# Two-layer decoder trunk: key chunks of the second layer turned by VectorE blocks and DRAM in place of TensorE

## What is computed

```python
def hgrn2_layer(h, norm_gain, w_in, o_gain, w_out, lower_bound):
    u = rms_norm(h, norm_gain)
    proj = u @ w_in                       # (1024, 4096)
    q, f_pre, i, gate = jnp.split(proj, ...)
    q = split_heads(jax.nn.silu(q), HG_HEADS)
    ...                                   # log_f from f_pre and the lower bound
    k_in = -jnp.expm1(log_f)
    o = hgrn2_chunkwise(q, log_f, k_in, split_heads(i, HG_HEADS))
    o = merge_heads(rms_norm(o, o_gain))
    return (o * jax.nn.silu(gate)) @ w_out

# inside a chunk step: S_t = diag(f_t) S_{t-1} + k_t i_t^T,  o_t = S_t^T q_t
new_state = (jnp.exp(g_last[:, :, 0, :])[..., None] * state
             + jnp.einsum('bhsd,bhsv->bhdv', kb * jnp.exp(g_last - g_cum), ib))
```

## Time and profile before

| | us |
|---|---|
| three executions | 1160.58, 1160.89, 1164.14 |
| median | 1160.89 |
| the profiled execution | 1160.32 |
| its span, first to last instruction | 1158.5 |
| TensorE busy in it | 1142.8 |
| VectorE busy | 826.1 |
| ScalarE busy | 416.6 |
| mean granted TensorE clock, as a share of 2.4 GHz | 1.000 |

### The profile page before, as it was taken

The page is one execution under the profiler, slowest core; times in us unless marked ns, Lnnn a source line. Parts: engine busy times, 40 slices in busy tenths (PEclk is TensorE's granted clock), DMA queues, the critical chain, the costliest instruction groups (busy, mean ns, idle before and its releaser), DMA issues. The chain is left out here.

```text
span 1158.5 us, 19342 instructions
## 1 busy us (share of the span) xinstructions
PE 1142.8 (99%) x7012; PEld 1049.0 (91%) x7012; DVE 826.1 (71%) x1620; ACT 416.6 (36%) x887; POOL 168.9 (15%) x360
## 2 busy tenths in 40 slices
PE   8999999999999999999999999999999999999998
PEld 7999998989898999988888999999999999999787
DVE  5768776878687877674444787888888888788421
ACT  5544544444544445442223122323232332222200
POOL 2412133222323212100004000000000000000000
PEclk9999999999999999999999999999999999999999
DMA  8243447474646421174622112324232331108441
GB/s 254 56 121 102 142 136 211 128 209 132 216 140 196 143 76 47 60 281 166 182 94 83 37 37 56 103 74 134 89 113 91 110 96 33 47 37 309 141 141 73
DMA packets 145211, 141.76 MB, mean 122 GB/s; under 512 B 19936, under 2 KB 117472, under 8 KB 145120
## 3 DMA queue, kind: packets, MB, share of 16 engines
q1 hardware_dynamic: 106336, 120.88, 32.0%
q10 hardware_dynamic: 38784, 19.67, 6.4%
HBM read 93.86 MB, written 46.66 MB: 121 GB/s over the span
## 5 line engine op out<-in xcount | busy, mean ns | idle before, releaser
L28 PE MATMUL p_proj<-w_qkv_hi,ut_hi 128*128 128x384 f32 x504 | 173.0, 343 | 5.9 <-DVE a_gated L1016 5.6
L30 PE MATMUL p_proj<-w_qkv_hi,ut_lo 128*128 128x384 f32 x504 | 169.1, 336 | 0.0
L29 PE MATMUL p_proj<-w_qkv_lo,ut_hi 128*128 128x384 f32 x504 | 168.7, 335 | 0.0
L28 PE MATMUL p_proj<-w_ig_hi,next_hi 128*128 128x256 f32 x512 | 145.5, 284 | 0.0
L29 PE MATMUL p_proj<-w_ig_lo,next_hi 128*128 128x256 f32 x512 | 143.1, 279 | 0.0
L30 PE MATMUL p_proj<-w_ig_hi,next_lo 128*128 128x256 f32 x512 | 143.0, 279 | 0.0
L28 PE MATMUL p_proj<-next_hi,w_qf_hi 128*128 128x512 f32 x282 | 113.2, 401 | 0.0
L30 PE MATMUL p_proj<-next_hi,w_qf_lo 128*128 128x512 f32 x282 | 110.1, 390 | 0.0
L29 PE MATMUL p_proj<-next_lo,w_qf_hi 128*128 128x512 f32 x282 | 109.9, 390 | 0.0
L941 DVE TENSOR_TENSOR_SCAN a_skip<-a_skip,a_diagonal 128x641 f32<-128x641 f32 (+3 forms) x64 | 87.7, 1370 | 30.4 <-ACT a_beta L760 30.4
L28 PEld LDWEIGHTS p_proj<-w_qkv_hi,ut_hi 128*128 128x128 f32 x504 | 94.8, 188 | 7.8 <-DVE a_gated L1016 6.4
(11 more groups left out here) (259 smaller groups left out, 2787.0 us busy)
## 6 DMA issues: line engine op xcount, KB each, us to landing
stage<-in_hg_w_in_dram SPq DMA_DIRECT2D x32, 512.0 KB, 4.4
stage<-in_sb_w_in_dram ACTq DMA_DIRECT2D x24, 512.0 KB, 5.4
w_out_hi_scratch<-m_in SPq DMA_DIRECT2D x32, 256.0 KB, 2.5
w_out_lo_scratch<-m_in SPq DMA_DIRECT2D x32, 256.0 KB, 2.8
m_in<-mixed_scratch SPq DMA_DIRECT2D x12, 448.0 KB, 5.8
a_gated<-in_x_dram SPq DMA_DIRECT2D x8, 512.0 KB, 3.7
m_in<-in_sb_w_out_dram SPq DMA_DIRECT2D x16, 256.0 KB, 3.9
ut_hi<-w_out_hi_scratch SPq DMA_DIRECT2D x8, 512.0 KB, 8.5
```

What stands on the lines that cost most here:

```text
L28: pe.matmul(out, w_hi, m_hi, start=start, stop=False, skip_group_check=True)
L29: pe.matmul(out, w_hi, m_lo, start=False, stop=False, skip_group_check=True)
L30: return pe.matmul(out, w_lo, m_hi, start=False, stop=stop, skip_group_check=True)
```

## The change

For heads 0 to 6 the transposes on TensorE and the copies on ScalarE go. In their place, in the same step:

1. VectorE, behind `chunk_keys`: one transpose of seven chunks (128 x 896) in blocks of 32 by 32, from `k_chunk` into the first 896 columns of `out_turned` (`flip_keys`). Each block is turned in itself; blocks that have to move to other partitions still lie on the old ones.
2. ScalarE's queue, in use 3 behind `place_last`: four stores (`store_keys`), one for each group of 32 partitions, 112 KB each, to DRAM in pieces of 32 floats. Each store has 896 pieces, the four have 3584.
3. ScalarE's queue, at the start of use 4: four reads (`read_keys`), each with 32 partitions of `k_turned` and 3584 contiguous bytes to a partition. ScalarE first waits for all four stores.
4. TensorE's `update` waits for the four reads (`k_landed`).

Head 7 keeps `turn_keys` and `copy_keys`. The DRAM area is `flips[0]` of layer 0, which is free by then. `mix_values` takes over the wait for `o_ready` from `turn_keys`.

```diff
+    RUN = (TILES - 1) * BLOCK
+    CARRIED_KEYS = 4 * RUN
...
+        by_token = k_flips.rearrange("p s -> (p s)")[0:BLOCK * 4 * CARRIED_KEYS]
+        by_token = by_token.rearrange("(i c) -> i c", i=BLOCK)
...
             def copy_keys(h):
 
                 for u in range(2):
-                    act.wait_ge(k_turned_done, 2 * h + u + 1)
-                    if not known_first(h):
-                        act.wait_ge(update_done, 2 * h)
+                    act.wait_ge(k_turned_done, u + 1)
+                    act.wait_ge(update_done, 2 * h)
...
+            def store_keys(h):
+
+                act.wait_ge(k_flipped, h + 1)
+                if not known_first(h):
+                    act.wait_ge(k_landed, 64 * h)
+                for group in range(4):
+                    act.dma_start(by_token.rearrange("i (c g j) -> i c g j", g=4, j=BLOCK)[:, :, group, :],
+                                  out_turned[group * BLOCK:(group + 1) * BLOCK, 0:CARRIED_KEYS].rearrange(
+                                      "p (c j) -> p c j", j=BLOCK)).then_inc(k_flip_stored, 16)
+
+            def read_keys(h):
+
+                if not known_first(h):
+                    act.wait_ge(update_done, 2 * h)
+                    act.wait_ge(sums_ready, TILES * h)
+                act.wait_ge(k_flip_stored, 64 * (h + 1))
+                for quarter in range(4):
+                    act.dma_start(flat(k_turned)[quarter * BLOCK:(quarter + 1) * BLOCK, 0:CARRIED_KEYS],
+                                  by_token[:, quarter * CARRIED_KEYS:(quarter + 1) * CARRIED_KEYS]
+                                  ).then_inc(k_landed, 16)
...
                     if projects and i in (1, 2):
                         split_hi(n, i + 1)
+                    if mixes and i == 4:
+                        read_keys(h)
                     if projects and i in (4, 5) and not last_head:
                         split_hi(n + 1, i - 4)
...
                     if mixes and projects and i == 3:
                         place_last(h, b)
-                    if mixes and i == 4:
-                        copy_keys(h)
+                        store_keys(h)
...
-                    dve.wait_ge(k_turned_done, 2 * h)
+                    dve.wait_ge(k_flipped, h)
                     dve.wait_ge(self_done, h)
...
+            def flip_keys(h):
+
+                dve.wait_ge(k_chunk_ready, h + 1)
+                if not known_first(h):
+                    dve.wait_ge(out_stored, 16 * h)
+                    dve.wait_ge(k_flip_stored, 64 * h)
+                dve.transpose(out_turned[:, 0:CARRIED_KEYS].rearrange("p (c s i) -> p s c i", c=4, i=BLOCK),
+                              k_chunk[:, 0:CARRIED_KEYS].rearrange("p (s c i) -> p s c i", c=4, i=BLOCK)
+                              ).then_inc(k_flipped, 1)
...
                         chunk_keys(h, b)
+                        flip_keys(h)
                         chunk_queries(h, b)
...
+                carried = h < HEADS - 1
                 for u in range(2):
-                    pe.wait_ge(k_turned_ready, 2 * h + u + 1)
+                    if carried:
+                        pe.wait_ge(k_landed, 64 * (h + 1))
+                    else:
+                        pe.wait_ge(k_turned_ready, u + 1)
...
                 pe.wait_ge(chunk_ready, h + 1)
+                if not known_first(h):
+                    pe.wait_ge(o_ready, TILES * h)
...
-                    if mixes and i == 3:
-                        turn_keys(h)
```

More of the change, by code:

```diff
@@ L126, in build_trunk @@
                    (hg_w_out[0], w_out_hi[1], w_out_lo[1]), next_hi, next_lo,
-                   w_qf_hi, w_qf_lo, w_ig_hi, w_ig_lo, parts, p_proj, p_pair, mixed[1], h1)
+                   w_qf_hi, w_qf_lo, w_ig_hi, w_ig_lo, parts, p_proj, p_pair, mixed[1], h1, flips[0])
         build_output_projection(nc, "l1", consts, stage, m_in, links[1], mixed[1], next_hi, next_lo, h1, out,
@@ L1619, in build_hgrn @@
 def build_hgrn(nc, c, stage, m_in, link, w, w_in, w_out, ut_hi, ut_lo,
-               w_qf_hi, w_qf_lo, w_ig_hi, w_ig_lo, parts, p_proj, p_pair, mixed, residual):
+               w_qf_hi, w_qf_lo, w_ig_hi, w_ig_lo, parts, p_proj, p_pair, mixed, residual, k_flips):
     L = len(LEVELS)
@@ L1701, in build_hgrn @@
         k_turned_ready = sem("k_turned_ready")
+        k_flipped = sem("k_flipped")
+        k_flip_stored = sem("k_flip_stored")
+        k_landed = sem("k_landed")
         update_done = sem("update_done")
@@ L2373, in finish @@
                 pe.wait_ge(last_placed, HEADS)
-                pe.wait_ge(k_turned_ready, 2 * HEADS)
+                pe.wait_ge(k_turned_ready, 2)
                 update(h, b, p_last)
```

## The result

The changed kernel takes **1177.74 us** (median of 4 runs, 1175.29 to 1180.19), the kernel before 1160.99 us beside it (4 runs, 1160.58 to 1164.14). The ratio is 1.0136, with a 95% interval of 1.0113 to 1.0159: slower by 1.4%. That lies inside the range, at its upper end, and in the direction of the rival *slow small writes*; the likeliest case of +1.2 us did not come, and the time is 13 times as far from the kernel before.

What follows compares the result with a forecast made beforehand. TensorE alone was taken to set the pace; the 6.2 us gain was lost to VectorE and DMA waits, 4 x 0.25 + 3 x 0.05 = +1.2 us on 1160.89, about 1162.1 us; 8-in-10 range 1160.0 to 1180.0.

Steps and rivals of the forecast that it cites:

- slow small writes: Rival: the stores' packets cost more than a read's or issues stall; at 28 ns, 24 us more, 1185; 40% in all.
- the likeliest case: Whole kernel: update and pair sum slightly late in heads 0 to 6, +1.2 us, about 1162.1 us.
- the prediction's own signs: Right: update and L2004 waits, flip 1.1 us, stores landing about 4.3 us. Wrong: period 56.0, update waits 3 us, or sigmoid waits.
- TensorE sets the pace; a microsecond is gained only if no wait appears: Heads 0 to 6: TensorE alone is the limit, so removed time counts only if nothing it waits for becomes late.
- Transposes, 0.89 us a head: TensorE after use 3's last matmul: removing seven transposes gains at most 0.89 us a head, 6.2 us in seven.
- Flip 1.11, VectorE 1.16 later, pair sum 0.22 late and 0.20 early: VectorE's transpose delays its queue; pair sum 0.22 us later in heads 1 to 4, 0.20 earlier in 0, 5, 6.
- VectorE catches up before the next head: VectorE between heads: idle times such as that of 1.81 us absorb the delay, so it doesn't add up.
- Stores landed after 4.3 us: Four stores on ScalarE's queue: 3584 packets at 13 ns; issued at about 737.6, landed at 741.9.
- Reads 1.3 + 2.6 us: Four reads after the stores: fourth issued 1.3 us later, landing 2.6 us after; 0.2 us added in heads 1 to 4.
- Heads are alike: Second layer: head 1 taken as the pattern, heads repeating every 56.87 us.
- Queue of ScalarE covered: Store issues ahead of the f sigmoids: up to 1.6 us of delay covered, as VectorE wants them only at 742.24.
- Tipping point, stores landing 0.6 us later than reckoned: Stores landing after about 742.5 make the update 0.5 us late and the kernel slower by over 0.3%.

Runs made afterwards that it cites:

- e1: Kernel before without the seven transposes and the copies in heads 0 to 6, nothing in their place (output wrong): 1158.11 us, ratio 0.9959.
- e2: e1 plus VectorE's transpose of 128 x 896 behind k_chunk, no stores or reads (carried state wrong): 1163.83 us, ratio 1.0013 to the kernel before.
- e8: Changed kernel with k_chunk and flip moved on VectorE to the end of use 2, ahead of the f scale: 1161.54 us, ratio 0.9995 to the kernel before.
- e4: Changed kernel with its four stores in rows of 3584 contiguous bytes (keys in wrong order): 1163.12 us, ratio 1.0012 to the kernel before.
- e9: Changed kernel with 30 small matmuls ahead of the first head, so instruction fetches fall elsewhere: ratio 1.0163 to the kernel before, two executions.
- e10: e8 with k_chunk and flip also ahead of the split of the last w_ig part: 1173.86 us, ratio 1.011 to the kernel before.
- e11: e8 with the stores in rows of 3584 bytes, as in e4 (keys in wrong order): 1157.2 us, ratio 0.9957 to the kernel before.
- e12: Changed kernel with TensorE's update and pair sum moved from behind use 4 to the middle of use 5: 1162.41 us, ratio 0.9999 to the kernel before.
- e3: e2 plus the four stores and four reads, read back into out_turned, TensorE not waiting (carried state wrong): 1163.01 us, ratio 1.0008 to the kernel before.
- e13: e8 with update and pair sum also in the middle of use 5 on TensorE: 1157.5 us, ratio 0.9957 to the kernel before, 10 runs.

## Why the prediction was right or wrong

The time lies in the range, but not for the reason that set the range's upper end. The sum gave +1.2 us and the ratio puts +15.8 beside it; the rival that the range was widened for had packets at 28 ns, and they took 13.6. That other causes came out at 1177.7 is luck. By the prediction's own signs the picture is mixed: the flip took 1.1 us, but the pair sum waited for VectorE nowhere, the stores landed after 5.0 us, and in two heads the update waited over 3 us.

- **TensorE sets the pace; a microsecond is gained only if no wait appears**: right, and the runs above are read by it.
- **Transposes, 0.89 us a head**: too large, 0.76 by e1. The distance to the next load was read as the price; the step of 0.23 us that a 512-column matmul leaves to the first load behind it was hidden under the transposes. Over seven heads, and with 0.84 us of wait in head 7, 4.5 us in place of 6.2.
- **Flip 1.11, VectorE 1.16 later, pair sum 0.22 late and 0.20 early**: right, 1.11 and +0.18 and -0.24 in e2. In the changed kernel itself this wait is not seen, since the update's wait covers it.
- **"VectorE catches up before the next head"**: failed at the last head, 1.44 us in e2. The idle time of 1.81 us that the sentence names was not usable where the flip stood, behind it. Put in front of it (e8), head 7 waits 0.4.
- **Stores landed after 4.3 us**: the failing step of the sum. Packet price 13.6 ns (13 taken); the fixed part was 2.0 us and not 1.35, as it was taken from one store and not from four issues of 0.68 us each; in all 5.0. e4 agrees: with the packets of the earlier trace rows, 1.15 us for all of them, its four stores take 3.3 us, which leaves 2.2. Beside it, the Trainium skill ("DMA: Bandwidth & Descriptors", Why small descriptors are slow) gave an estimate of 10.5 ns; the row's 13.6 speaks against using it here.
- **Reads 1.3 + 2.6 us**: 1.3 + 2.8 in head 1, 1.3 + 2.4 in heads 0, 5 and 6, nearly right; the 0.2 us for the w_out stores beside them were about 0.4 in head 1 and 1.0 to 1.3 in heads 3 and 4. Both together put the update of a quiet head 0.4 to 1.4 us late, in place of 0.05 to 0.25: 4.0 us in heads 0, 1, 2, 5 and 6, where the sum had 0.65.
- **Heads are alike**: wrong, and the largest term. I took head 1 for all. Heads 3 and 4 cost 8.7 us where the sum had 0.5: some 2 us more wait each, of which 1.2 to 1.4 where an instruction fetch meets the stores (e9 moves it) and the rest where the late reads meet the w_out stores (read from the trace, not tested by a run), and two falls of the clock, up to 3.4 us. Such fetches are in the trace of the kernel before too; the prediction did not look at what else uses the DMA engines.
- **Queue of ScalarE covered**: right. The f sigmoids came at 742.94, 5.3 us after k_chunk's start, 0.9 later than in the earlier trace rows (the one ahead of its first row stood at 739.53), and VectorE's next f scale, at 744.67, came after their end (744.03).
- **Tipping point, stores landing 0.6 us later than reckoned**: right. They landed 0.7 later, and with it nearly all of the quiet heads' loss is there (5 x 0.7 + 0.65 = 4.2 us by the sum, 4.0 measured); the rival's price of 3.5 us a head was too high for these and too low for heads 3 and 4 (4.4 and 4.3), which lost it through another mechanism.

Left open: why a wait of 1.9 us was followed by a clock fall in one head and one of 3.50 us in another was not. And a kernel whose executions differ (1158.4 to 1166.5 in e8) may do so by such falls, but not by them alone: the two quickest of e8 have a granted clock of 1.000 and the slowest 0.997, yet one of 1164.8 us has 0.999.

## What to carry to other kernels

A result that travels by DMA needs a margin against its worst landing, not its median: count the issues, the packets, what else may stand on a single one of the engines, and what a late start will meet, since a chain of stores then reads waits for the slowest engine twice. If the margin is missing, look for idle time ahead of the producer and for a later place of the reader. Earlier is not better by itself (e10); here each of the two in the right place gave back about 16 us, and both together turned a loss of 1.4% into a gain of 0.4%. And before an operation is priced by the distance it takes up, ask what its neighbours will show when it is gone.

## What the runs showed of the hardware

- 128-byte packets from on-chip memory to DRAM took 13.6 ns each, about as the reads of the earlier trace rows did (13); issues of 896 packets followed each other by 0.59 to 0.72 us, those of 32 rows of 3584 bytes by 0.34 to 0.48 (e4).
- The first packet moved 1.24 us after the first issue's start. The Trainium skill ("DMA: Bandwidth & Descriptors", Latency and other measured facts) has about 0.6 us for this; here it was twice that, and 0.8 us with 32 long rows to an issue (e4).
- Stores take longer beside large loads: the small-packet ones took 5.0 us alone, 6.0 beside 0.8 MB of loads (e8), 8.3 beside 1 MB (e10). Long rows are not spared: 3.3 us alone, 4.6 beside the loads of e8 (e11).
- One 16 KB instruction packet held one DMA engine for 0.9 to 1.7 us, and one of 0.92 us delayed a store's landing by 1.4 us (head 3).
- In the heads, six falls of TensorE's clock to 0.50 for 3.4 us stood beside waits of 1.89, 3.49 (changed kernel), 2.13 (e8), 2.35 (e9), 2.19 and 3.22 us (e10). None stood beside waits of 3.50 (changed kernel), 1.99, 2.04 (e10) and 1.96 us (e12), and none in the heads of e1, e2, e3, e4, e11 and e13, where the longest wait was 1.63 us (e3).
